# Two output tiles of a convolution branch and two of a Fourier branch, moved to the values' banks and spread over the attention

## What is computed

```
uf, uc, q, k, v = split_heads(hn_lat @ w_in)
mix_lat = concatenate([fourier_mix(uf, w_fourier),        # f = fftn(uf).real ; f @ w
                       conv_module(uc, ...),              # silu(layer_norm(conv(v))) @ pw_w + pw_b
                       neighbourhood_attention(q, k, v, k_ctx, v_ctx, na_rpb)])
h_lat = h_lat + g1 * (mix_lat @ w_out)
```

## Time and profile before

| | |
|---|---|
| median of 3 runs | 1760.62 us (1759.85 to 1761.23) |
| profiled execution, own time | 1760.18 us |
| its span in the profile | 1758.1 us |
| TensorE, VectorE, ScalarE busy | 1717.3, 1105.4, 647.6 us |
| step of the attention, steady (1296.40 to 1308.85, four steps) | 3.11 us |
| granted clock of TensorE over the span | 0.995 |

### The profile page before, as it was taken

How to read it: one execution, slowest core, us unless ns; L and a number is a source line. 1 busy time by engine, 2 the same in 40 slices (tenths; PEclk the granted TensorE clock), 3 DMA queues, 4 the chain that set the end, 5 groups by cost and what they waited for, 6 DMA issues and landing times.

```text
span 1758.1 us, 23599 instructions
## 1 busy us (share of the span) xinstructions
PE 1717.3 (98%) x8325; PEld 1405.4 (80%) x8325; DVE 1105.4 (63%) x1924; ACT 647.6 (37%) x939; POOL 76.4 (4%) x63
## 2 busy tenths in 40 slices
PE   5999999999999999999999999999999999999998
PEld 3788888888778867887888888898867888888887
DVE  6777677655656655549978973569685553434343
ACT  3442222233236663344322334342375342323241
POOL 2000000011000000110000000200000200000002
PEclk8999999999999999999999999999999999999999
DMA  8776566433323301445666642455201233333321
GB/s 278 219 231 196 187 194 200 132 89 98 103 75 95 96 1 48 136 140 178 205 204 186 183 120 78 122 152 120 73 1 33 64 111 92 106 86 107 92 88 48
DMA packets 360716, 218.39 MB, mean 124 GB/s; under 512 B 11576, under 2 KB 358724, under 8 KB 360644
## 3 DMA queue, kind: packets, MB, share of 16 engines
q1 hardware_dynamic: 360644, 217.46, 41.6%
HBM read 215.34 MB, written 2.11 MB: 124 GB/s over the span
## 4 chain that ended last, share of the span: by engine, by line
PE 92%; DVE 4%; ACT 1%; issue 1%; SPq 1%; DMA 1%; DVEq 0%; ACTq 0%
PE bank L666 26%; PE bank L668 26%; PE bank L667 26%; PE bank L696 2%; PE bank L697 2%; PE bank L700 2%; PE bank L797 1%; PE bank L786 1%; PE bank L856 1%; DVE GACC L1454 1%; PE bank L718 1%; PE bank L831 1%; DMA GBUF<-in_w_ada 1%; PE bank L1018 0%; DVE STAT L1589 0%
## 5 line engine op out<-in xcount | busy, mean ns | idle before, releaser
L666 PE MATMUL bank<-H_HI,W_HI 128*128 128x512 f32 x1304 | 508.4, 390 | 1.4 <-DVE W_LO L1430 1.2
L667 PE MATMUL bank<-H_LO,W_HI 128*128 128x512 f32 x1304 | 507.4, 389 | 0.0
L668 PE MATMUL bank<-H_HI,W_LO 128*128 128x512 f32 x1304 | 507.4, 389 | 0.0
L1116 ACT ACTIVATE W_HI<-RAW 128x1024 fp32r<-128x1024 f32 x279 | 293.9, 1057 | 478.5 <-PE bank L668 455.7
L1430 DVE TENSOR_TENSOR W_LO<-RAW,W_HI 128x1024 fp32r<-128x1024 f32 x282 | 345.8, 1227 | 85.6 <-ACT W_HI L1116 76.0
L666 PEld LDWEIGHTS bank<-H_HI,W_HI 128*128 128x128 f32 x1304 | 244.2, 187 | 54.1 <-issue 2.9
L666 PE MATMUL bank<-A_HI,W_HI 128*128 128x512 f32 x736 | 287.0, 390 | 0.0
L668 PE MATMUL bank<-A_HI,W_LO 128*128 128x512 f32 x736 | 286.4, 389 | 0.0
L667 PE MATMUL bank<-A_LO,W_HI 128*128 128x512 f32 x736 | 286.4, 389 | 0.0
L667 PEld LDWEIGHTS bank<-H_LO,W_HI 128*128 128x128 f32 x1304 | 244.2, 187 | 51.5 <-issue 0.2
L668 PEld LDWEIGHTS bank<-H_HI,W_LO 128*128 128x128 f32 x1304 | 244.2, 187 | 51.4
(11 more groups left out here) (270 smaller groups left out, 1555.3 us busy)
## 6 DMA issues: line engine op xcount, KB each, us to landing
RAW<-in_ffn_w SPq DMA_DIRECT2D x120, 512.0 KB, 4.8
GBUF<-in_w_ada SPq DMA_DIRECT2D x33, 1024.0 KB, 6.8
RAW<-in_mlp_w SPq DMA_DIRECT2D x64, 512.0 KB, 3.8
RAW<-in_w_in SPq DMA_DIRECT2D x57, 512.0 KB, 3.9
GBUF<-in_ada_w SPq DMA_DIRECT2D x24, 1024.0 KB, 7.0
RAW<-in_w_out SPq DMA_DIRECT2D x16, 512.0 KB, 3.6
RAW<-in_ffn_w SPq DMA_DIRECT2D x16, 384.0 KB, 3.2
RAW<-in_w_branch SPq DMA_DIRECT2D x8, 512.0 KB, 3.6
```

The lines of the kernel that those rows point to most:

```text
L666: pe.matmul(dst, w_hi, x_hi, start=first and i == 0, stop=False)
L667: pe.matmul(dst, w_hi, x_lo, start=False, stop=False)
L668: mm = pe.matmul(dst, w_lo, x_hi, start=False, stop=last and i == len(blocks) - 1)
L1116: act.activation(strip_of(W_HI, slot), strip_of(RAW, slot), ACT.Copy).then_inc(hi_ready, 1)
```

## The change

The four tiles get banks 6 and 7, the two of the values. Both convolution tiles stay in step 1, in the banks 6 and 7. The first Fourier tile is made in step 2, in bank 7, once `mixed` is at 6; the second in step 3, in bank 7 again, once `mixed` is at 7. The wait for `mixed` at 8 moves to step 6, ahead of the first value product in bank 7. On ScalarE and VectorE `meanwhile` is now called in every step, and the work on each Fourier tile stands in its step. Banks 4 and 5 are left to the transposes.

```diff
+OUT_TILES = {1: (0, 1), 2: (2,), 3: (3,)}
@@ TensorE
+                def output_tile(b, w, x, m):
+
+                    for c in range(2):
+                        mm = pe.matmul(bank[b][:, :], w[:, (2 * c + m) * P:(2 * c + m + 1) * P], chunk(x, c), start=c == 0, stop=c == 1)
+                    mm.then_inc(mix_done, 1)
+
                 def make_outputs(step):
 
                     if step == 1:
                         pe.wait_ge(bias_ready, H)
                         pe.wait_ge(act_ready, 2)
-                        for i, (w, x) in enumerate(((PW, ACC), (WF, FT))):
-                            for m in range(2):
-                                for c in range(2):
-                                    mm = pe.matmul(bank[4 + 2 * i + m][:, :], w[:, (2 * c + m) * P:(2 * c + m + 1) * P], chunk(x, c),
-                                                   start=c == 0, stop=c == 1)
-                                mm.then_inc(mix_done, 1)
+                        output_tile(6, PW, ACC, 0)
+                        output_tile(7, PW, ACC, 1)
+                    if step == 2:
                         pe.wait_ge(mixed, 6)
+                        output_tile(7, WF, FT, 0)
                     if step == 3:
+                        pe.wait_ge(mixed, 7)
+                        output_tile(7, WF, FT, 1)
+                    if step == TT + 2:
                         pe.wait_ge(mixed, 8)
@@ ScalarE and VectorE, attend
-                    if p == 1:
-                        meanwhile()
+                    meanwhile(p)
@@ ScalarE (VectorE alike, with mix_hi, mixed and A_LO)
-                def outputs():
-                    for i, m in enumerate((2, 3, 0, 1)):
+                def outputs(step):
+                    for i in OUT_TILES.get(step, ()):
+                        m, src = (2, 3, 0, 1)[i], bank[7 if i else 6][:, :]
                         act.wait_ge(mix_done, i + 1)
                         if m < 2:
-                            ins = act.activation(chunk(A_HI, m), bank[4 + i][:, :], ACT.Copy)
+                            ins = act.activation(chunk(A_HI, m), src, ACT.Copy)
```

More of the change, by code:

```diff
@@ L1242, in mixer1, with values @@
                     act.activation(chunk(QT, n // 2), bank[4 + n % 4][0:DQ, :], ACT.Copy).then_inc(turn_act, 1)
-                def values():
-                    for n in range(2 * H, 2 * H + TT, 2):
+                def values(step):
+                    for n in range(2 * H, 2 * H + TT, 2) if step == 1 else ():
                         act.wait_ge(turned, n + 1)
@@ L1328, in mixer2 @@
                                    scale=COL1[:, V_LNG + c:V_LNG + c + 1]).then_inc(act_ready, 1)
-                def outputs():
-                    for i, m in enumerate((2, 3, 0, 1)):
+                def outputs(step):
+                    for i in OUT_TILES.get(step, ()):
+                        m, src = (2, 3, 0, 1)[i], bank[7 if i else 6][:, :]
                         act.wait_ge(mix_done, i + 1)
                         if m < 2:
-                            ins = act.activation(chunk(A_HI, m), bank[4 + i][:, :], ACT.Copy)
+                            ins = act.activation(chunk(A_HI, m), src, ACT.Copy)
                         else:
-                            ins = act.activation(chunk(A_HI, m), bank[4 + i][:, :], ACT.Identity,
+                            ins = act.activation(chunk(A_HI, m), src, ACT.Identity,
                                                  bias=COL1[:, V_PWB + m - 2:V_PWB + m - 1])
@@ L1728, in mixer1, with values @@
                     dve.tensor_copy(chunk(KT, n // 2), bank[4 + n % 4][0:DQ, :]).then_inc(turn_dve, 1)
-                def values():
-                    for n in range(2 * H + 1, 2 * H + TT, 2):
+                def values(step):
+                    for n in range(2 * H + 1, 2 * H + TT, 2) if step == 1 else ():
                         dve.wait_ge(turned, n + 1)
@@ L1846, in outputs @@
                         if m < 2:
-                            ins = dve.tensor_tensor(lo, bank[4 + i][:, :], hi, ALU.subtract)
+                            ins = dve.tensor_tensor(lo, src, hi, ALU.subtract)
                         else:
-                            ins = dve.scalar_tensor_tensor(out=lo, in0=bank[4 + i][:, :], scalar=COL1[:, V_PWB + m - 2:V_PWB + m - 1],
+                            ins = dve.scalar_tensor_tensor(out=lo, in0=src, scalar=COL1[:, V_PWB + m - 2:V_PWB + m - 1],
                                                            in1=hi, op0=ALU.add, op1=ALU.subtract)
```

## The result

| | before | changed |
|---|---|---|
| median | 1759.93 us (20 runs, 1759.46 to 1761.23) | 1764.05 us (20 runs, 1762.73 to 1767.67) |
| ratio | | 1.0024, 95% interval 1.0017 to 1.0030 |
| profiled execution, span | 1760.18, 1758.1 us | 1764.58, 1762.7 us |
| first scores to transposes of pair 3 | 19.76 us | 23.34 us |
| first scores to the projection | 63.19 us | 66.76 us |

The change costs 4.1 us, or 0.24%. 3.58 of it is seen in the profile in the place where it was forecast. The distance in the fourth row starts at the first S(0) (1282.86 in before) and ends at T(3), which the earlier trace rows show at 1302.62.

A forecast was written before the change was run, and what follows sets the result against it. TensorE, busy 98%, bounds the kernel, with no slack behind the attention. From 1290.99, laps of 6.29 and 6.21 plus 3.03 put pair 3's transposes at 1306.52 against 1302.62: 1760.62 + 3.9 = 1764.5 us, range 1762.4 to 1766.0.

The forecast's parts named there:

- S(0): Neighbourhood attention on TensorE: the scores of head pair 0.
- T(3): Transposes of pair 3's probabilities on TensorE, the forecast's milestone: 1302.62 us before, 1306.52 forecast; steady pitch from there.
- The mechanism: Two laps of waits through the attention's engines: +3.9 us, own range +3.4 to +4.3, chance 0.77.
- What bounds it: TensorE, busy 98%, with no slack behind the attention; finished head pairs' outputs absorb nothing, so its delay is the kernel's.
- Convolution tiles, moved wait, order of the rest: 0: Attention: banks 6 and 7 for convolution tiles, the Fourier wait moved to step 6, and later order cost nothing.
- The lead of 2.46 us on VectorE: Bias and maximum of pair 2 start 2.46 us earlier, but the lead is lost; rival that it lives on: 1758.2, 0.04.
- F0: First of the Fourier branch's two tiles; in bank 7 it waits for the convolution tile's A_LO until 1290.99.
- A lap, 6.29 us: Attention, from one Fourier tile's wait to its A_LO's end: links sum to 6.29 us, the second lap 6.21.
- The idle stretches: TensorE idle about 1.4 and 2.3 us ahead of the Fourier tiles; VectorE 2.8 and over 2 ahead of their A_LO.
- The clock: Rival: TensorE's granted clock falls to 1.2 GHz in the attention's new gap, +3.1, in all +7.0: 1767.6 us; chance 0.04.
- The rival of covered waits: Only TensorE's 12.04 us of attention work stands in line, no engine holding it up: +0.5, 1761.1 us; chance 0.10.
- the ring: Attention's cycle of waits: F tile, transposes, PT copies, exponentials, A_HI, A_LO, next F tile; gone through twice.

The follow-up runs named there:

- the version with four banks and early copies: Against before: four banks kept, scores of pair 2 ahead of the Fourier tiles, their ScalarE copies heading step 2; 1758.53 us, ratio 0.9990.
- the kernel with one bank: Against the changed kernel: all four tiles in bank 7, one in each of steps 1 to 4; 1767.90 us, ratio 1.0046 to before.
- the kernel with the early copy: Against the changed kernel: each Fourier tile's A_HI copy moved to the head of its step on ScalarE; 1760.12 us, ratio 0.9999 to before.
- the kernel with the filled gap: Against the changed kernel: eight products of constants into bank 6 ahead of step 3's wait; 1763.58 us, ratio 1.0024 to before.

## Why the prediction was right, point by point

- *The number.* Forecast 1764.5 us (1762.4 to 1766.0), which is +3.9; measured 1764.05, which is +4.1. The mechanism gave 3.58 of it. The rest came from elsewhere, as the points below say, and that the total lies so near the forecast is in part luck.
- *What bounds it.* A delay of the attention is a delay of the kernel: it lost 3.58 us by T(3) and 3.57 by the projection, and from there to the end before has 412.05 us and the changed kernel 411.76. Nothing was given back at the finished pairs of heads, as argued.
- *Convolution tiles, moved wait, order of the rest: 0.* Right. Their A_LO ended 8.14 us behind the first scores, in before 8.13.
- *The lead of 2.46 us on VectorE.* It was there, and it was lost at the A_LO of F0, as argued. That it can be kept is shown by the version with four banks and early copies. What TensorE's work allows was the limit I named for the changed kernel, and that version has another order of work.
- *A lap, 6.29 us.* Measured 6.15. The links were 0.05 us instead of 0.10 from A_LO to the tile, 1.82 instead of 1.88 for the tile, 0.64 instead of 0.69 to the PT copies, 2.29 and 0.65 + 0.70 behind that. Three of these links were shorter than in the rows of before that I took them from: over two laps and the way to T(3) 0.3 us. So the sum was +3.9, with 3.58 measured. The mechanism's own range, +3.4 to +4.3, holds it (by the two terms named for it, its lower end should have been +3.3).
- *The idle stretches.* 1.30 and 2.22 us on TensorE (forecast 1.4 and 2.3), 2.61 twice on VectorE (2.8, and over 2).
- *The clock.* I gave its fall in the new gap a chance of 0.04 and took it for all or nothing. It falls in some executions (one of five profiles), and costs 1.5 us then, not 3.1. I had taken a window with gaps and a clock of 1.00 as evidence against it, but one profile is one draw. I had also taken it that the length of an idle stretch decides. The runs don't bear that out: the clock fell behind 0.7 and 1.6 us in the kernel with one bank, and stayed at 1.00 behind 3.37 us at the start of the changed kernel's profile, where in before it fell.
- *The rival of covered waits.* Its price was +0.5, and the kernel with the early copy comes near it: distance +0.26, time +0.1. It needed a move of the copy that the change doesn't have.
- *Open.* The medians lie 4.1 to 4.8 us over before in three comparisons. 3.57 is the ring. The remaining 0.5 to 1.3 isn't explained. The spans of the five profiles of the changed kernel lie 4.34 us over the two of before in the mean: 3.56 are the ring, 0.30 the one fallen clock in this attention, and 0.50 a later beginning, behind falls of the clock at the program's start and in the first block in the two latest of them. Whether the last part belongs to the change or to chance, five profiles against two can't tell. A fall in one execution of five hardly moves a median either, and the kernel with the filled gap was 0.78 us faster, which its interval doesn't separate from nothing.

## What to carry to other kernels

A tile that must wait for the evacuation of the one before is not dear for the wait, but for the ring that it closes. List, engine by engine, what stands ahead of the evacuating copy, and ask whether any of it begins only behind products that TensorE issues after the tile. If so, from one tile to the next a full lap passes (6.15 us here, against a steady step of 3.11), however short the work; moving the copy ahead of its neighbours (one place on ScalarE here) gave back 3.3 of 3.6 us. The same question, asked of the copies that were there all along, gave 1.5 us in this attention and 0.7 in the first block's. Count the laps before counting banks.

## What was not expected of the hardware

- The granted clock fell behind a gap of 2.2 us in one execution and not in four others of the same program, and behind 0.7 and 1.6 us, with 1.14 us of work between them, in the kernel with one bank. A tile of four instructions then takes 3.4 to 3.5 us instead of 1.98. It also fell once in the first block's attention, behind 1.43 and 0.86 us, for 1.3 us, and stayed up behind 3.37 us near the program's start. The same program with the same gaps falls or doesn't from one execution to the next.
- Work in the attention repeats to about 0.03 us from one execution to the next as long as the clock stays up, while its beginning varies by up to 2 us. In the two cases followed up, most of this came from the clock: in the first 60 us, and in the first block's attention. To compare two kernels by their profiles, distances within the stage are worth more than spans.
